# Score maxima of the next head pair and two projections woven into the score steps of a window attention, with two buffers of query parts and one of exponentials

## The reference, cut to what matters

```python
A_HEADS_2 = 8
A_KV_HEADS = 2
A_WINDOW = 128

def _sink_probs(parts, sink):
    ...
    p = jax.nn.softmax(jnp.concatenate(list(parts) + [snk], axis=-1), axis=-1)
    return p[..., :-1]

def _window_gqa_sink(q, k, v, kc, vc, sink):
    ...
        valid = (jnp.abs(qpos[:, None] - kpos[None, :]) <= W) & (kpos >= 0)[None, :] & (kpos < S)[None, :]
        s_loc = jnp.einsum('bqkgd,bskd->bkgqs', qn, kn).astype(jnp.float32) * scale
        s_loc = jnp.where(valid, s_loc, NEG)
        s_ctx = jnp.einsum('bqkgd,bckd->bkgqc', qn, kc).astype(jnp.float32) * scale
        p = _sink_probs([s_loc, s_ctx], sink).astype(v.dtype)
```

## Time and profile before

| | |
|---|---|
| runs, median (lowest to highest) | 4742.05 us (4739.6 to 4753.11), 3 runs |
| profiled execution, device time | 4743.4 us |
| its span, first to last instruction | 4741.5 us |
| PE busy, whole span | 3994.4 us, 84% |
| the four passes (first peak to next stage) | 2212.85 to 2591.31 us, 378.5 us |
| PE busy in them | 300.6 us |

### The profile page before, as it was taken

The page is one execution under the profiler, slowest core; times in us unless marked ns, Lnnn a source line. Parts: engine busy times, 40 slices in busy tenths (PEclk is TensorE's granted clock), DMA queues, the critical chain, the costliest instruction groups (busy, mean ns, idle before and its releaser), DMA issues. The chain is left out here.

```text
span 4741.5 us, 44431 instructions
## 1 busy us (share of the span) xinstructions
PE 3994.4 (84%) x18448; PEld 3121.0 (66%) x18448; DVE 2288.8 (48%) x3662; ACT 1445.2 (30%) x2369; POOL 422.1 (9%) x398
## 2 busy tenths in 40 slices
PE   4899987887979999987877878876878998788877
PEld 2688865655758888865655657654756676565556
DVE  4899246555542222345454444545444555334344
ACT  3221234343121111123433333333233444222231
POOL 2112100001010000001000222211010000000000
PEclk9899878898989999998888889877978997888888
DMA  2133230003401111121000000002200000000012
GB/s 76 59 108 132 98 112 24 18 18 111 147 31 49 48 46 42 53 76 36 20 20 30 18 15 14 19 15 78 77 30 26 26 22 14 28 5 8 8 52 91
DMA packets 67514, 225.23 MB, mean 48 GB/s; under 512 B 7848, under 2 KB 11944, under 8 KB 67312
## 3 DMA queue, kind: packets, MB, share of 16 engines
q1 hardware_dynamic: 43056, 132.68, 8.5%
q0 software_dynamic: 20800, 77.12, 4.5%
q10 hardware_dynamic: 3456, 12.58, 0.7%
HBM read 180.95 MB, written 37.74 MB: 46 GB/s over the span
## 5 line engine op out<-in xcount | busy, mean ns | idle before, releaser
L1920 PE MATMUL PS<-m,m 128*128 128x512 f32 (+4 forms) x4216 | 1750.9, 416 | 356.8 <-DVE m L2255 63.7
L1921 PE MATMUL PS<-m,m 128*128 128x512 f32 (+4 forms) x4216 | 1643.6, 390 | 0.0
L1922 PE MATMUL PS<-m,m 128*128 128x512 f32 (+4 forms) x4216 | 1641.9, 390 | 0.0
L1920 PEld LDWEIGHTS PS<-m,m 128*128 128x128 f32 (+1 forms) x4216 | 832.4, 198 | 741.0 <-issue 287.7
L1922 PEld LDWEIGHTS PS<-m,m 128*128 128x128 f32 (+1 forms) x4216 | 839.7, 199 | 157.8
L1921 PEld LDWEIGHTS PS<-m,m 128*128 128x128 f32 (+1 forms) x4216 | 843.4, 200 | 126.3 <-issue 2.9
L2516 DVE TENSOR_TENSOR m<-PS,m 128x512 fp32r<-128x512 f32 x352 | 240.3, 689 | 418.4 <-ACT m L2179 417.2
L2252 DVE TENSOR_TENSOR m<-m,m 128x1024 fp32r<-128x1024 f32 (+4 forms) x203 | 212.4, 1046 | 425.8 <-ACT m L2085 425.2
L2179 ACT CAST m<-PS 128x512 fp32r<-128x512 f32 x352 | 203.8, 584 | 366.1 <-PE PS L2007 365.6
L2007 PE MATMUL PS<-m,m 128*128 128x128 f32 x1408 | 252.2, 308 | 69.2 <-DVE m L2512 29.6
L2085 ACT CAST m<-m 128x1024 fp32r<-128x1024 f32 (+4 forms) x235 | 213.0, 907 | 260.8 <-PE PS L1922 188.8
(11 more groups left out here) (194 smaller groups left out, 3702.4 us busy)
## 6 DMA issues: line engine op xcount, KB each, us to landing
m<-in_w SPq DMA_DIRECT2D x220, 512.0 KB, 3.3
g_scratch<-m ACTq DMA_DIRECT2D x24, 512.0 KB, 2.8
m<-g_scratch POOLq DMA_DIRECT2D x24, 512.0 KB, 4.7
m<-in_w SPq DMA_DIRECT2D x32, 256.0 KB, 2.6
x_scratch<-m POOLq DMA_DIRECT2D x2, 4096.0 KB, 12.3
y_scratch<-m POOLq DMA_DIRECT2D x15, 512.0 KB, 2.9
m<-y_scratch POOLq DMA_DIRECT2D x15, 512.0 KB, 5.7
y_scratch<-m POOLq DMA_DIRECT2D x7, 640.0 KB, 3.2
```

The source lines that it names most:

```text
L1920: pe.e.engine.matmul(o, L[0], X[0], start=start, stop=False)
L1921: pe.e.engine.matmul(o, L[0], X[1], start=False, stop=False)
L1922: return pe.e.engine.matmul(o, L[1], X[0], start=False, stop=stop)
```

## The change

The maxima of pass 0 are taken ahead of the loop, with `eq1` between them. In pass `j` the 11 score steps now carry, through `hook`, the maxima of pass `j`+1: two peaks behind the cross of each step from step 4 on. They also carry, as `fill`, the projection `eg` of this pass and (for `j` below 2) the query projection `eq(j+2)`. `turned` of the next queries stands in step 1 and their split in step 3, into a second pair of buffers (`qs`). To make room `P` has one buffer (`Crossed(..., 1)`), the window mask is loaded apart, and the exponential of the sink uses the scratch `G`. `tops` and the store of its rows (`rows_out`) come behind the last step, ahead of the last two gathers; the rows are loaded back (`rows_in`) at the call of the next `run`. `fq0` is no longer projected here but with `fk0` and `fv0` in the next stage, and rotated there by matmul.

```diff
-    def run(self, chunks, keys, queries, ext, sm, values, after, v_after, fill=None, extra=None, settled=None):
+    def run(self, chunks, keys, queries, ext, sm, values, after, v_after, fill, tail, settled, extra=None, hook=None, end=None):
...
                 x = self.cross(segments, keys, queries, ext, sm, masks, after)
                 after = []
-                n = -(-fill.left // total) if fill else 0
...
+                if hook:
+                    hook(i)
+                n = -(-max(0, fill.left - tail) // (total - i))
+                i += 1
+                fill.pull(n // 2)
+                behind.append((x, q0, w, k == 0, k == len(steps) - 1))
                 if len(behind) > 2:
                     one_behind()
...
+                fill.pull(n - n // 2)
         self.rest(x)
-        if fill:
-            fill.drain()
+        if end:
+            end()
         while behind:
+            fill.pull(-(-fill.left // len(behind)))
             one_behind()
...
-        at = Crossed(p, mem, [(0, 1), (2, 3)], (4, 5), [6, 7])
+        at = Crossed(p, mem, [(0, 1), (2, 3)], (4, 5), [6, 7], 1)
...
+        def rows_in():
+            return [move(ext[64 * h:64 * h + 3, :], x_d[:, 10 * h:10 * h + 10, :].rearrange("t r c -> t (r c)"),
+                         m_free + made_t + ext_free) for h in range(2)]
...
+        for _ in peak_steps(0):
+            q_fill.pull(2)
+        q_fill.drain()
+        rows_out(0)
         for j in range(4):
+            zg_t, g_steps = z_linear(f"eg{j}", zg, 1.0, at.fill_banks)
...
+            fill = Fill(fill_steps(), 48 if j < 2 else 24)
             if j == 0:
...
+                fill.pull(10)
+            peaks = peak_steps(j + 1)
+
+            def hook(i):
+                x = (j + 1) % 2
+                if j == 3:
+                    return
+                if i == 1:
+                    q_done[:] = turned(zq, nxt_t[j + 1])
+                if i == 3:
+                    q_t[x] = split(qs[x][0][:, :], qs[x][1][:, :], zq[:, :], q_done)
+                if i > 3:
+                    next(peaks, None)
+                    next(peaks, None)
+
+            def end():
+                if j < 3:
+                    for _ in peaks:
+                        pass
+                    rows_out(j + 1)
...
-                   rows_t + made_t, tok_t + made_t, None, sinks, settled)
-            at.stop()
+                   rows_in() + made_t + q_t[j % 2] + k_t, tok_t + made_t, fill, 10, settled, sinks, hook, end)
             ext_free = [at.last_cross, at.last_pv]
             z_free = [y_store(j, zg, TC, y_t)]
...
-        for _ in next_steps(CHE, {"k": "fk0", "v": "fv0"}, None):
+        for _ in next_steps(CHE, {"q": "fq0", "k": "fk0", "v": "fv0"}, None):
             pass
-        ev["q"] = fq_events
         done = []
-        for _ in rotate_steps("k", None, done):
+        for _ in rotate_steps("qk", None, done):
             pass
```

More of the change, by code:

```diff
@@ L666, in run @@
         behind = []
+        i = 0
         def one_behind():
@@ L676, in run @@
         for q0, w, steps in chunks:
-            for i, (segments, masks) in enumerate(steps):
+            for k, (segments, masks) in enumerate(steps):
                 if x:
@@ L1440, in schedule @@
                 m = p.id()
[L1441 to L1443 removed]
+                p.add("make", n=m, after=k_t + [t_w],
+                      parts=[(vh[:, :, 64:128], ones, 1024.0), (vl[:, :, 64:128], ones, 0.0),
+                             (idr[:, :], ident, 1.0), (winr[:, :], at.G[:, 0:384], 1.0), (ext[:, 0:T], tabs[:, 0, :], 0.0),
+                             (ext[:, T:TC], tabs[:, 0, 0:256], 0.0), (sk[:, :], ident, 0.0)]
                       + [(sm[a:b, :], ident[a:b, a:a + 1].to_broadcast([64, 128]), 1.0) for a, b in halves])
                 made_t = [(S.evac, (m, "made"))]
+                at.u_free = at.u_free + made_t
                 m = p.id()
@@ L1489, in schedule, with peak_steps @@
         chunks = [(q0, w, [(seg, masked(seg)) for seg in steps]) for q0, w, steps in window_steps]
[L1490 to L1498, removed]
+        m_free, ext_free, z_free = [], [], tok_t
+        top = []
+        def peak_steps(j):
+            qh = qs[j % 2][0]
+            after = q_t[j % 2] + k_t
             for b in range(10):
@@ L1523, in schedule @@
-            zg_t, steps = z_linear(f"eg{j}", zg, 1.0, at.fill_banks)
-            if j == 0:
-                p.add("ready", on="act", after=tok_t)
-            else:
-                p.add("ready", on="act", after=z_free)
-            g_fill = Fill(steps, 24)
-            g_fill.pull(8)
-            q_done = turned(zq, nxt_t)
-            g_fill.drain()
+                    top[:] = [at.peak([[(256 * i, 256, qh[rows_of(h), 128 * (b - 1 + i):128 * (b + i)], kh[rows_of(h), T:TC])
+                                        for i in range(2)] for h in range(2)],
+                                      [[(0, 512, 2, None, mc[:, 10 * h + b - 1:10 * h + b + 1])] for h in range(2)], after, m_t)]
@@ new lines, in schedule, with fill_steps @@
+        p.add("ready", on="act", after=q_t[0])
+        nxt_t, q_done = {}, []
+        nxt_t[1], steps = z_linear("eq1", zq, 0.125, at.fill_banks)
+        at.start()
+        q_fill = Fill(steps, 24)
+        for _ in peak_steps(0):
+            q_fill.pull(2)
+        q_fill.drain()
+        rows_out(0)
+        for j in range(4):
+            zg_t, g_steps = z_linear(f"eg{j}", zg, 1.0, at.fill_banks)
+            def fill_steps():
+                p.add("ready", on="act", after=z_free)
+                yield from g_steps
+                if j < 2:
+                    p.add("ready", on="act", after=q_t[(j + 1) % 2])
+                    nxt_t[j + 2], steps = z_linear(f"eq{j + 2}", zq, 0.125, at.fill_banks)
+                    yield from steps
+            fill = Fill(fill_steps(), 48 if j < 2 else 24)
+            if j == 0:
+                fill.pull(10)
[16 more added lines that the diff above has]
+                    rows_out(j + 1)
@@ L2738, in constants @@
     j = np.arange(384)
-    out["win"] = np.where(np.abs(p[:, None] - j[None, :] + 128) <= 128, 0.0, NEG)
+    win = np.where(np.abs(p[:, None] - j[None, :] + 128) <= 128, 0.0, NEG).astype(np.float32)
     c = np.arange(64)
```

78 lines of the change are left out of this document (32 added, 46 removed).

## The result

| | kernel before | changed kernel |
|---|---|---|
| median (lowest to highest), same job | 4747.6 us (4739.6 to 4756.7), 4 runs | 4801.3 us (4791.3 to 4812.9), 4 runs |
| ratio | | 1.0117, 95% interval 1.0093 to 1.0141 |
| span of the profiled execution | 4741.5 us | 4811.0 us |
| first peak to the next stage's first scores | 418.1 us | 472.4 us |

The change makes the kernel slower by 54 us, 1.2%. I had forecast slower, by 30: 4772, with a range from 4738 to 4794. The measured time is above the range. The profiled execution of the changed kernel is the slowest of its four (4812.9 us), and the trace of the kernel before is from one of 4743.4 us; so the two spans differ by more than the medians.

A forecast was written before the change was run, and what follows sets the result against it. PE, busy 300.6 of 378.5 us, was taken as the bound, so waits decide. Work plus waits gave passes of 391.7 us (+13.2); with the next stage's `fq0` +13.9 and rotation +3.3, +30.4 in all: 4772 us, range 4738 to 4794.

The forecast's parts named there:

- three boundaries: Between passes, PE's first cross waits for row loads queued on POOL behind the result's store: 14.4 us each, before 10.9.
- step 7: Behind the first settle, the exponential waits for step 6's rest with one buffer `P`: PE waits 8.6 us, 9.3 in pass 2.
- step 4: First peak of the new queries waits behind their cast and rest: 2.9 us, 6.3 in pass 2.
- second peaks: Steps 5, 6, 8 and 9: the second peak waits 1.0 us for the exponential of the cross just issued, 4.0 a pass.
- `tops`: End of the peaks: the earlier 2.09 us wait was to go, as five k-steps are pulled behind it.
- pass 3, inside: Last pass, without peaks: settle and the one buffer, chaining exponential, cast and rest, cost 6.7 us.
- next stage, growth: Next stage gains `fq0`, +13.9 us, and the rotation of q behind that of k, +3.3.
- The work of a pass: PE work of a full pass: projections 27.8, score steps 33.3, thirteen peaks 5.5, in all 66.6 us.
- restart: Behind a long PE wait, matmuls run at the 1.2 GHz level for some 3.5 us, costing about 1.7 us.
- 1 and 2: Rivals: waits inside steps mostly vanish, half gone gives 4740 (chance 0.17); all vanish and clock stays high, 4707 (0.09).
- Rival 4: Boundary bounded by the row loads alone, not POOL's store order: 14.4 falls to about 5 us, giving 4744; chance 0.04.
- Rival 3: With one buffer each exponential waits for the previous step's rest, adding 1 us to each of 27 steps: 4799; chance 0.12.

The follow-up runs named there:

- e1: Changed kernel with the two loads of the next pass's rows ahead of the result's store on POOL; ratio 1.0090 to the kernel before.
- e6: Changed kernel with the edits of e1, e2 and e3 together; ratio 1.0027 to the kernel before.
- e2: Changed kernel with the rest of the newest step issued ahead of a settle on DVE; ratio 1.0079 to the kernel before.
- e3: Changed kernel with a step's two peaks apart, one behind the first half of its k-steps, one behind its gather; ratio 1.0062 to the kernel before.
- e7: e6 plus six k-steps of `eg` ahead of the first cross of passes 1 to 3; ratio 1.0031 to the kernel before.
- e9: e8 plus eight k-steps of the next projection ahead of the first peak of passes 1 to 3; 4718.7 us, ratio 0.9936 to the kernel before.
- e8: Kernel before with the next queries' split behind a pass's last cross, ahead of the last gathers and settle; ratio 0.9972 to the kernel before.
- e5: Kernel before with `fq0` projected and rotated in the next stage instead of pass 3; ratio 1.0023 to the kernel before.

## Where the prediction was right, and the step that failed

| term | forecast | measured |
|---|---|---|
| three boundaries | 3 x 14.4 | 14.27, 14.28, 14.19 |
| step 7 | 8.6, 9.8, 9.3 | 8.78, 8.77, 8.04 |
| step 4 (two waits added) | 2.9, 2.9, 6.3 | 2.8, 2.2, 3.7 |
| second peaks, a pass | 4.0 | 5.6, 4.2, 4.6 |
| `tops` | 0 | 2.25, 1.55, 2.34 |
| pass 3, inside | 6.7 | 3.9 |
| end of the stage | 13.4 | 13.4 |
| next stage, growth | 17.2 | 18.7 |
| head, passes 0 to 3 | 36.2, 92.0, 101.9, 90.9, 70.7 | 35.5, 100.7, 109.2, 95.4, 73.3 |

**The waits were right.** But for `tops`, their places, their releasers and their sum came as the forecast had them. It had 117.5 us of waits in passes 0 to 3 and some 4 in the head, about 122; PE was idle for 119.0. That the sums agree to 3 us is in part luck: 6.1 us at `tops` and 2.3 at the second peaks were not in it, and step 4, step 7 and pass 3 came out 3.4, 2.1 and 2.8 us lower. The rule of the Trainium skill that spoke against the placing (DMA: Bandwidth & Descriptors, "Rules for kernel authors": issue early, wait late) is borne out: the boundary waits 14.3 us, and 3.4 in e1, which issues early. The 2.0 us of fixed cost that the same page of the Trainium skill gives ("Anatomy of one DMA") would have given boundaries of 13.2 us, an estimate by that figure. The trace has 14.2 to 14.3, and 3.1 us from issue to landing of these loads.

**The step that failed is "The work of a pass", 66.6 us.** I built PE's work from clean pieces, most of them at 2.4 GHz, and added 1.7 us for each long wait. The whole forecast of 391.7 us thus holds 391.7 - 122 = 270 us of PE work. But the earlier trace rows, the first row I read, has 300.55 us of it; less a `fq0` at 13.9 that is 286.7. The same 1652 matmuls took 295.0 in the changed kernel. So 17 us of it stood in the earlier trace rows before the prediction, another 8 came on top, at a lower granted clock (0.84 against 0.88), and 3 us less of waits leave the 22 by which the passes were forecast too short. Built as a difference from the earlier trace rows, with the same waits, the sum is 378.5 - 77.95 - 13.9 + 122 = 408.7, or +30.2 for the passes; with +17.2 for the next stage and the 1.4 of the profiled run that is 4789 us, inside my own range, 12 below the measured 4801. (Another 5.5 us of the miss are none of the change: the kernel before had a median of 4742.05 in the runs that I started from and 4747.6 beside the changed kernel.) The absolute sum was checked against nothing: the same method gives 66.6 + 19.5 of waits + 3.4 for two restarts = 89.5 us for pass 1 of the kernel before, which takes 93.4. Four times these 3.9 us are 16 of the 17.

**The price of a restart is not one number.** I took 1.7 us for each. Behind the boundary to pass 1 the granted clock is at its 1.2 GHz level up to 2357.12:

```profile
2353.11 0.79 PE L1956 MATMUL PS<-m,m 128*128 128x512 f32 x1
2353.70 0.63 PE L1957 MATMUL PS<-m,m 128*128 128x512 f32 x1
...
2356.69 0.63 PE L1958 MATMUL PS<-m,m 128*128 128x512 f32 x1
...
2357.72 0.40 PE L1958 MATMUL PS<-m,m 128*128 128x512 f32 x1
```

The cross ahead of them took 2.08 us, and 1.20 for the same eight matmuls at 2358.04. With it the lower level lasted 6 us here, and some 3 were lost. Behind step 7's wait in pass 0 a k-step takes 0.39 us again at 2306.24, so there it lasted 4.6 us at most. And the clock falls behind short waits too. In step 4 of pass 1 PE waits 0.57 and 1.62 us, and the half-width k-steps behind them take 0.42 us up to 2384.4, against 0.27 at 2388:

```profile
2376.32 0.39 PE L2065 MATMUL PS<-m,m 64*128 64x256 f32 x2 [0.57 <-DVE m L2291]
2378.32 0.69 PE L2065 MATMUL PS<-m,m 64*128 64x384 f32 x2 [1.62 <-ACT m L2247]
...
2379.32 0.42 PE L1957 MATMUL PS<-m,m 128*128 128x256 f32 x1
...
2387.99 0.27 PE L1958 MATMUL PS<-m,m 128*128 128x256 f32 x1
```

A price per wait does not follow from this either. e6 has 46 us less idle time than the changed kernel in the passes and 292.6 us of PE work against 295.0; e1, e2, e3 and e7, with the same 1652 matmuls, have 296.6, 289.9, 293.1 and 294.0. So the 8 us are within what single traces differ by, and what part of them the added waits caused stays open.

**The `tops` wait did not go.** I wrote that five k-steps are pulled behind it; what covers a wait has to stand ahead. The last peaks and `tops` follow each other with nothing between, so DVE's last maxima are waited for as before: 6.1 us at three `tops` that the forecast had at nothing.

**The rivals.** The small waits did not vanish (1 and 2). Rival 4's mechanism, the loads alone, is e1: it did not happen. Rival 3 gave a time, 4799, that is near the measured one, but by luck: it adds 27 us of waits to the forecast's, and PE was idle for 3 us less than the forecast had. Its chain is there on ACT and lengthens some waits of second peaks, which came to 14.3 us against 12.0. "Slower", to which I gave 0.68, came; the range ended 7 us short because it held doubts on the waits only, and none on PE's work.

## What to carry to other kernels

Make a forecast as a difference from a measured window: keep its PE busy time, clock and all, and change only the waits; and let the method first reproduce the kernel before. In such a loop ask of every engine's queue what the newly placed instruction stands behind: the loads behind a store that waits for the settle, a rest behind the settle, a maximum behind the settle cost 33, 20 and 22 us of PE waits here (not to be added up: the last takes the place of the one before it). Independent k-steps are a fixed stock: eight of them moved to a wait of 6.7 us gave another 17 us by the ratio (e9 against e8), six moved to a wait of 3.4 us gave nothing (e7 against e6). So put them at the longest wait that is left.

## What the runs showed of the hardware that I had not expected

The first part of e5 has the same PE instructions as the kernel before, and still a different duration. Windows of the kernel before, then of e5, from the first peak to the first cross:

```profile
2212.80:2252.00 39.20, 37.06 (x181) 0.95 0.15 43
```

```profile
2215.10:2257.10 42.00, 39.91 (x181) 0.87 0.13 40
```

181 matmuls take 37.06 us at a granted clock of 0.95 and 39.91 at 0.87. Over the head and two passes the difference is 2.8 + 0.5 + 4.0 = 7 us, with nothing changed there. So a difference of some 7 us between two single traces is no evidence for a cause. The 13 us that lie behind the changed stretch, over some 2100 us of the same code, are none either.
